# A hybrid decoder trunk in one kernel: the last value pair by halves, value tiles on VectorE, the last round's rows by output weight, and the first weight half split ahead of x

## The reference

```python
z = gelu(x @ w_in + b_in)                 # 1024 -> 2 * 3072, exact gelu
u, v = split(z, 2)
v = layer_norm(v, ln_g, ln_b)             # over all 3072; the last chunk's rows of v are outputs too
sg = chunk_spatial_gate(v, w_s, b_s)      # per chunk of 128 tokens and per head: lower-triangular W_s @ v + b_s
y = (u * sg) @ w_out                      # 3072 -> 1024
x = layer_norm(ALPHA * x + y, ln1_g, ln1_b)
```

## Time and profile before

| what | us |
| --- | --- |
| median of 3 runs | 1261.38 |
| lowest, highest | 1260.33, 1261.75 |
| the profiled execution | 1261.01 |
| its span, first to last instruction | 1259.0 |
| PE busy in it | 1211.5 |
| DVE busy | 908.9 |
| ACT busy | 626.7 |
| POOL busy | 260.8 |

### The profile page before, as it was taken

How to read it: one execution, slowest core, us unless ns; L and a number is a source line. 1 busy time by engine, 2 the same in 40 slices (tenths; PEclk the granted TensorE clock), 3 DMA queues, 4 the chain that set the end, 5 groups by cost and what they waited for, 6 DMA issues and landing times.

```text
span 1259.0 us, 19311 instructions
## 1 busy us (share of the span) xinstructions
PE 1211.5 (96%) x7563; PEld 1094.7 (87%) x7563; DVE 908.9 (72%) x1215; ACT 626.7 (50%) x756; POOL 260.8 (21%) x270
## 2 busy tenths in 40 slices
PE   7999988999999997999999999999999999999998
PEld 6888888999999996888778699999998888877698
DVE  4654788687877875889889786445534889888793
ACT  4332444444444542478888663211221478888651
POOL 2311022442514422022332001000002022232100
PEclk9999999999999998999999999999999999999999
DMA  8456326675957755379999563222422369999512
GB/s 303 146 185 210 118 71 178 144 193 122 204 156 156 192 138 210 143 270 373 372 385 342 194 185 106 70 99 68 134 67 89 143 236 365 381 387 355 213 51 76
DMA packets 99582, 246.47 MB, mean 196 GB/s; under 512 B 10694, under 2 KB 55886, under 8 KB 87216
## 3 DMA queue, kind: packets, MB, share of 16 engines
q1 hardware_dynamic: 68976, 182.20, 40.7%
q0 software_dynamic: 30528, 63.20, 18.1%
HBM read 212.50 MB, written 49.62 MB: 208 GB/s over the span
## 4 chain that ended last, share of the span: by engine, by line
PE 66%; DMA 14%; DVE 11%; ACT 5%; issue 3%; POOL 0%; SPq 0%; DVEq 0%; POOLq 0%; ACTq 0%
PE ps L2073 13%; PE ps L2075 12%; PE ps L2074 12%; DMA w_raw<-in_moe_w_gate_up 9%; PE ps L2124 3%; PE ps L2126 3%; PE ps L2125 3%; DVE w_lo L1382 3%; PE ps L2482 2%; ACT w_hi L981 2%; PE ps L2484 2%; PE ps L2483 2%; PE ps L2175 1%; PE ps L2288 1%; PE ps L2290 1%
## 5 line engine op out<-in xcount | busy, mean ns | idle before, releaser
L1382 DVE TENSOR_TENSOR w_lo<-w_raw,w_hi 128x2048 fp32r<-128x2048 f32 (+1 forms) x133 | 290.4, 2191 | 64.3 <-ACT w_hi L981 57.2
L2073 PE MATMUL ps<-x_hi,w_hi 128*128 128x288 f32 (+2 forms) x784 | 234.8, 299 | 4.2 <-DVE g_full L1538 2.3
L981 ACT ACTIVATE w_hi<-w_raw 128x2048 fp32r<-128x2048 f32 (+1 forms) x121 | 219.7, 1826 | 36.6 <-PE ps L2075 16.1
L2075 PE MATMUL ps<-x_hi,w_lo 128*128 128x288 f32 (+2 forms) x784 | 232.3, 296 | 0.0
L2074 PE MATMUL ps<-x_lo,w_hi 128*128 128x288 f32 (+2 forms) x784 | 232.2, 296 | 0.0
L2073 PEld LDWEIGHTS ps<-x_hi,w_hi 128*128 128x128 f32 x784 | 148.8, 190 | 6.2 <-issue 4.9
L2074 PEld LDWEIGHTS ps<-x_lo,w_hi 128*128 128x128 f32 x784 | 148.9, 190 | 0.1
L2075 PEld LDWEIGHTS ps<-x_hi,w_lo 128*128 128x128 f32 x784 | 148.8, 190 | 0.0
L2073 PE MATMUL ps<-g_hi,w_hi 128*128 128x288 f32 x384 | 114.6, 298 | 1.6 <-DVE g_lo L1517 0.7
L2075 PE MATMUL ps<-g_hi,w_lo 128*128 128x288 f32 x384 | 113.3, 295 | 0.0
L2074 PE MATMUL ps<-g_lo,w_hi 128*128 128x288 f32 x384 | 113.1, 295 | 0.0
(11 more groups left out here) (347 smaller groups left out, 2656.5 us busy)
## 6 DMA issues: line engine op xcount, KB each, us to landing
w_raw<-in_moe_w_gate_up SPq DMA_DIRECT2D x34, 1024.0 KB
w_raw<-in_moe_w_down SPq DMA_DIRECT2D x32, 1024.0 KB
w_raw_more<-in_moe_w_gate_up SPq DMA_DIRECT2D x30, 1024.0 KB
w_raw<-in_a_w_in SPq DMA_DIRECT2D x23, 1024.0 KB
w_raw<-in_a_w_out SPq DMA_DIRECT2D x12, 1024.0 KB
w_raw<-in_b_w_in SPq DMA_DIRECT2D x12, 1024.0 KB
sum_scratch<-out_stage POOLq DMA_DIRECT2D x40, 288.0 KB, 7.1
w_raw<-in_ple_w_gate SPq DMA_DIRECT2D x8, 1024.0 KB
```

The source lines that it names most:

```text
L981: act.activation(unit_of(whi, d), raw_unit(d), ACT.Copy).then_inc(hi_done, 1)
L1382: dve.tensor_tensor(unit_of(wlo, d), raw_unit(d), unit_of(whi, d).bitcast(f32), ALU.subtract).then_inc(split_done, 1)
L2073: pe.matmul(out, sh, mh, start=first, stop=False)
L2075: ins = pe.matmul(out, sl, mh, start=False, stop=final)
```

## The change

It has four parts.

- **Start.** ScalarE and VectorE split the first half of the first weight unit before x of token tile 0.
- **Last value pair.** TensorE runs the last pair by halves, like pair 0, with its loop over the pairs written out. Its first unit is free after the first half (`wait_used`). ScalarE and VectorE split unit U_A, make its sums and split these at the end of pair 4 instead of in pair 5, and in pair 5 the second unit (U_A + 2) with its sums. ScalarE copies the first product before the square root of the variance.
- **Value tiles.** ScalarE's and POOL's operations on tiles 3 and 4 go in every round; VectorE normalises all five. In round 0 the five stand between the combinations, and the first two spatial products stand together behind the second product of `jj` 1.
- **Last round's rows.** The wait for the second output unit moves behind the products of the first output half of both row tiles; the second half's follow in one piece.

The rest is counts: one increment of `rs_ok` is gone.

```diff
--- before.py
+++ after.py
@@ -555,7 +555,8 @@
             elif d >= 4:
-                eng.wait_ge(vps_done, it * (NT * step // 2) + NT * (d // 2 - 1))
+                n, a = divmod(d - 4, 2)
+                eng.wait_ge(vps_done, it * (NT * step // 2) + (NT * (n + 1) if n < VP - 1 else NT * n + 1 + NT * a))
@@ -864,15 +865,6 @@
-            def v_affine(rnd, i):
-                t, v = tok(i), vc[:, i, :] if i < NT - 1 else vcs[0:TS, :]
-                pool.wait_ge(act_scaled, KT + 2 * rnd + i - 2)
-                ch.link(pool.tensor_tensor(v, v, gb[0:t, 0, :], ALU.mult))
-                pool.tensor_tensor(v, v, gb[0:t, 1, :], ALU.add).then_inc(vn_ok, 1)
-
-            pool.wait_ge(vc_ld, 64)
-            for i in range(3, NT):
-                v_affine(0, i)
             for rnd in range(AR):
@@ -883,10 +875,6 @@
                         add_sum(rnd, mo)
-                        if mo == 3:
-                            pool.wait_ge(vc_ld, 64 * (rnd + 2))
-                            for i in range(3, NT):
-                                v_affine(rnd + 1, i)
@@ -981,6 +969,8 @@
+            act.wait_ge(fh_ld, 16)
+            act.activation(whi[:, 0, 0:UNIT // 2], raw[:, 0, 0:UNIT // 2], ACT.Copy).then_inc(fh_ok, 1)
             for i in range(NT):
@@ -988,8 +978,6 @@
                 if i == 0:
-                    act.wait_ge(fh_ld, 16)
-                    act.activation(whi[:, 0, 0:UNIT // 2], raw[:, 0, 0:UNIT // 2], ACT.Copy).then_inc(fh_ok, 1)
                     act.wait_ge(wld[0], 16)
@@ -1029,16 +1017,15 @@
                         elif i == 0:
-                            first_hi(U_A)
-                        else:
-                            sum_hi(U_A + 1)
+                            first_hi(a_entry(0, 2))
                     k = 3 * n - 3 + (i - 1 if i < 2 else i - 2)
...
                         combined_hi(i - 3)
-                if n == VP - 1:
-                    first_hi(a_entry(0, 2))
+                if n == VP - 2:
+                    first_hi(U_A)
+                    sum_hi(U_A + 1)
@@ -1047,9 +1034,6 @@
                 v_pair(n)
-            act.wait_ge(rs_ok, 1)
-            act.activation(rstd[:, :], rstd[:, :], ACT.Sqrt).then_inc(sq_ok, 1)
-
             def u_gelu(u, part):
@@ -1070,11 +1054,6 @@
-            def v_centred(rnd, i):
-                t, v = tok(i), vc[:, i, :] if i < NT - 1 else vcs[0:TS, :]
-                act.wait_ge(vc_ld, 64 * (rnd + 1))
-                act.activation(v, v, ACT.Identity, bias=nmr[0:t, i:i + 1], scale=rstd[0:t, i:i + 1]).then_inc(act_scaled, 1)
-
             def first_product(u):
@@ -1083,11 +1062,8 @@
                 u = 2 * rnd
-                first_product(u)
-                if rnd == 0:
-                    act.wait_ge(rs_ok, 3)
-                    for i in range(3, NT):
-                        v_centred(0, i)
+                if rnd:
+                    first_product(u)
                 sum_hi(a_entry(rnd, 3))
@@ -1110,13 +1086,14 @@
                         sum_hi(a_entry(rnd + 1, 1))
-                        for i in range(3, NT):
-                            v_centred(rnd + 1, i)
                     if mo == 5:
...
                 act.wait_ge(xi_st[j], 64)
+            first_product(0)
+            act.wait_ge(rs_ok, 1)
+            act.activation(rstd[:, :], rstd[:, :], ACT.Sqrt).then_inc(sq_ok, 1)
             for rnd in range(AR):
...
@@ -1381,6 +1358,11 @@
+            def half_lo(done, c0):
+                dve.wait_ge(done, 1)
+                return dve.tensor_tensor(wlo[:, 0, c0:c0 + UNIT // 2], raw[:, 0, c0:c0 + UNIT // 2], whi[:, 0, c0:c0 + UNIT // 2].bitcast(f32), ALU.subtract)
+
+            half_lo(fh_ok, 0).then_inc(fh_ok, 1)
             for i in range(NT):
@@ -1388,9 +1370,7 @@
                 if i == 0:
-                    for c, s in ((fh_ok, slice(0, UNIT // 2)), (hi_done, slice(UNIT // 2, UNIT))):
-                        dve.wait_ge(c, 1)
-                        dve.tensor_tensor(wlo[:, 0, s], raw[:, 0, s], whi[:, 0, s].bitcast(f32), ALU.subtract).then_inc(fh_ok if c is fh_ok else split_done, 1)
+                    half_lo(hi_done, UNIT // 2).then_inc(split_done, 1)
                 if i == 3:
@@ -1448,7 +1428,7 @@
                         dve.wait_ge(v_st[i // 4], n * 16)
-                    dve.wait_ge(vps_done, NT * n + i + 1)
+                    dve.wait_ge(vps_done, NT * n + i + 1 + (n == VP - 1))
                     ins = dve.tensor_tensor(vst[:, i, :], v_bank(i), v_bias_row(n), ALU.add)
@@ -1456,24 +1436,22 @@
                         lo(2 * n + 2 + i // 2)
-                    if n == VP - 1 and i == 0:
-                        combined_lo(1)
-                    if n == VP - 1 and i in (1, 3):
-                        if i == 1:
-                            first_lo(U_A)
-                            sums(U_A)
-                        else:
-                            lo(U_A + 1)
                     if i >= 1:
                         v_stats(n, i - 1)
+                    if n == VP - 1 and i == 1:
+                        first_lo(a_entry(0, 2))
+                    if n == VP - 1 and i == 2:
+                        sums(a_entry(0, 2))
                     if n == VP - 2 and i < 2:
...
                     combined_lo(0)
-                if n == VP - 1:
-                    first_lo(a_entry(0, 2))
+                    combined_lo(1)
+                    first_lo(U_A)
+                    sums(U_A)
+                    lo(U_A + 1)
@@ -1540,17 +1518,21 @@
                 combined(u, 0)
+                if rnd == 0:
+                    v_norm(0)
                 combined(u, 1)
                 if rnd == 0:
-                    sums(a_entry(0, 2))
+                    v_norm(1)
                 combined(u, 2)
-                if rnd:
+                if rnd == 0:
+                    v_norm(2)
+                else:
                     lo(a_entry(rnd, 3))
...
                 if rnd == 0:
-                    for i in range(3):
-                        v_norm(i)
+                    v_norm(3)
+                    v_norm(4)
                 combined(u, 5)
@@ -1587,7 +1569,8 @@
                 lo(d + 1)
-                v_norm(2)
+                for i in range(2, NT):
+                    v_norm(i)
                 first_lo(d + 2)
@@ -1602,7 +1585,6 @@
             dve.wait_ge(rs_ok, 2)
-            dve.scalar_tensor_tensor(out=nmr[:, :], in0=mv[:, :, 0], scalar=-1.0, in1=rstd[:, :], op0=ALU.mult, op1=ALU.mult).then_inc(rs_ok, 1)
             dve.wait_ge(vc_ld, 64)
...
@@ -2155,10 +2137,16 @@
             small_turns()
-            v_pair(1)
-            with pe.Fori(0, VP // 2 - 1) as it:
-                for j in range(2):
-                    v_pair(2 + j, it, 2)
+            for n in range(1, VP - 1):
+                v_pair(n)
+            for a in range(2):
+                pe.wait_ge(split_done, U_A - 1 + a)
+                for i in range(NT):
+                    if a == 0:
+                        pe.wait_ge(vz_done, NT * (VP - 2) + i + 1)
+                    ins = v_half(VP - 1, a, i)
+                    if a or i == NT - 1:
+                        ins.then_inc(vps_done, 1)
             pe.wait_ge(ones_ok, 1)
@@ -2208,8 +2196,9 @@
                         strassen(rnd, jj, n)
-                        if rnd == 0 and jj and n in (1, 2):
-                            spatial(rnd, n - 1)
+                        if rnd == 0 and jj and n == 1:
+                            spatial(rnd, 0)
+                            spatial(rnd, 1)
                         if jj and n == 4:
@@ -2384,14 +2373,14 @@
                     row_turns(1)
-                    pe.wait_ge(split_done, d + 2)
+                    pe.wait_ge(split_done, d + 1)
                     for k0, k1 in ((0, 2), (2, 3), (3, 4)):
...
                         for i in range(2):
-                            for h in range(2):
-                                ins = row_products(i, h, range(k0, k1))
-                            if k1 == ROUND:
-                                ins.then_inc(mt_done, 1)
+                            row_products(i, 0, range(k0, k1))
+                    pe.wait_ge(split_done, d + 2)
+                    for i in range(2):
+                        row_products(i, 1, range(ROUND)).then_inc(mt_done, 1)
                 p_turns(0)
```

More of the change, by code:

```diff
@@ L1273, in norm @@
                     t = tok(i)
-                    act.wait_ge(rs_ok, 3 + n2 + i + 1)
+                    act.wait_ge(rs_ok, 2 + n2 + i + 1)
                     act.activation(xtok[0:t, i, :], xtok[0:t, i, :], ACT.Identity, bias=nmr[0:t, i:i + 1], scale=rstd[0:t, i:i + 1]).then_inc(nz_ok, 1)
@@ L1633, in norm_of @@
                     ch.link(dve.reciprocal(rstd[0:t, i:i + 1], rstd[0:t, i:i + 1]))
-                    dve.wait_ge(rs_ok, 3 + n1 + i + 1)
+                    dve.wait_ge(rs_ok, 2 + n1 + i + 1)
                     dve.scalar_tensor_tensor(out=xtok[0:t, i, :], in0=xtok[0:t, i, :], scalar=rstd[0:t, i:i + 1], in1=lnp[0:t, 1, :],
```

(4 more changed lines are left out.)

## The result

The median of five runs is 1252.51 us (1251.87 to 1253.47), against 1261.38 for the kernel before, measured beside it: a ratio of 0.9928 [0.9916, 0.9940], 8.9 us less. The forecast was 1252.6. The profiled execution of the kernel after took 1253.47, the slowest of the five, with a span of 1251.4; the traces therefore differ by 7.6 us, 1.3 less than the medians.

A forecast was written before the change was run, and what follows sets the result against it. TensorE, busy 96% of the span, bounds the kernel, plus its stops. 0.8 + 6.2 + 0 + 1.8 = 8.8 us off 1261.01 gives 1252.2, with 0.37 for the median 1252.6; range 1251 to 1254 (45%).

The forecast's parts named there:

- A: Start: splitting the first weight half ahead of x lets TensorE's first product start at 9.2 instead of 10.03, 0.8 us.
- B: Last value pair and round 0: fifth product of the second column starts at 191.9 instead of 198.15, 6.2 us.
- VectorE's new wait of 2 us: Last value pair: VectorE waits 2 us before tile 0's bias, which goes 1.1 us late; its bank isn't needed before 170.
- The two idle pieces: Round 0: TensorE idles 0.95 us before the spatial products and 1.0 us before the next product.
- clock drop: Round 0 rival: the clock falls there as well, 1.65 us lost again, 1254.2; chance 10%.
- The rival in which B's stop only moves: Round 0: sums, tiles and low parts still queue on VectorE; if 4 us later than counted, 1256.6; chance 5%.
- the drain behind a table load: ScalarE's square root: the skill's rule makes the load about 2.66 us, not 1.28, giving 1253.5; prediction said the trace disagrees.
- C: Value tiles, rounds 1 to 5: VectorE's two extra tiles, 2.9 us per round, are covered by its waits; 0 us.
- The slower rival: Rounds 1 to 5: VectorE becomes the bound, 15 us on the path, 1267.6; chance 3%.
- D: Last round's rows: row tile 0 turned at 489.0 instead of 493.51, 4.5 us, less 2.65 for half clock: 1.8 net.
- The rival in which the clock stays up: Last round's rows: no clock drop behind the longer gap, 11.5 us in all, 1249.9; chance 20%.
- The one with the longer slow stretch: Last round's rows: 16 transposes don't bring the clock back and run at half speed; D is 0, 1254.4; chance 17%.

The follow-up runs named there:

- e1: The kernel after with the start as before (first weight half no longer split ahead of x); median 1253.83 us.
- e12: The kernel before with only layer norm's parameters scaled by VectorE instead of POOL, in both layers; median 1261.82 us, ratio 0.9997.
- e3: The kernel before with only the new start and the new order of the last round's rows; median 1258.68 us.
- e10: The kernel after with ScalarE's copy of the first product behind the square root again; median 1254.59 us.
- e4: The kernel after with value tiles 3 and 4 of rounds 1 to 5 on ScalarE and POOL again; median 1252.83 us.
- e5: The kernel after with unused products of ones keeping TensorE running ahead of the turnings of side inputs and row tile 0; median 1251.57 us.
- e7: e6 with TensorE turning row tile 0 ahead of the side inputs; median 1247.69 us.
- e9: e6 with unused identity products on TensorE at the start, three calls before x lands and five behind its transposes; median 1245.84 us.
- e2: The kernel after with the last round's output product waiting for both weight units again; median 1255.09 us.
- e6: The kernel after with layer norm's parameters scaled by VectorE instead of POOL, in both layers; median 1247.06 us.

## Why the prediction was right, step by step

**A, the start: 0.8 predicted, 1.5 in the trace.** The mechanism is as told. ScalarE and VectorE do the half first, and x after it:

```profile
6.10 1.06 ACT L973 ACTIVATE w_hi<-w_raw 128x1024 fp32r<-128x1024 f32 x1 [4.01 <-DMA w_raw<-in_a_w_in]
7.06 1.06 ACT L979 ACTIVATE x_hi<-ps 128x512 fp32r<-128x512 f32 x2
7.19 1.23 DVE L1363 TENSOR_TENSOR w_lo<-w_raw,w_hi 128x1024 fp32r<-128x1024 f32 x1 [7.19 <-ACT w_hi L973]
...
8.33 1.28 DVE L1371 TENSOR_TENSOR x_lo<-ps,x_hi 128x512 fp32r<-128x512 f32 x2
...
9.07 0.80 PE L2106 MATMUL ps<-w_hi,x_hi 128*128 128x512 f32 x1 [2.36 <-DVE x_lo L1371]
```

The first product came at 9.07 (9.2 predicted). The other 0.5 was not in the sum: TensorE starts at half clock (0.63 us for a product of 512 columns, later 0.39), and in the kernel after the clock rose at about 12.4 instead of 14.5. This is read from the matmuls' own times; the column of the granted clock stands at 1.00 from 9 to 16 us in both traces and doesn't show it. I had treated the slow stretch as part of the fixed work. But the extra 0.5 is not the change's. In the nine traces with the new start and nothing added in front, the first product comes at 8.83 to 9.26 and the first sample product at 25.21 to 26.73, on average 26.0. In the three with the old start (before, e1, e12) these are 9.95 to 10.06 and 26.35 to 27.64, on average 27.0. So A is worth 1.0 at both places. What decides when the clock rises no run here shows.

**B, the last pair and round 0: 6.2 predicted, 6.5 in the trace** (8.03 at the fifth product less the start's 1.51), and B and C together 6.2 to 6.7 by e3. The chain:

```profile
157.56 2.29 DVE L1359 TENSOR_TENSOR w_lo<-w_raw,w_hi 128x2048 fp32r<-128x2048 f32 x1 [1.98 <-ACT w_hi L1010]
159.89 0.69 DVE L1432 TENSOR_TENSOR v_stage<-ps,v_bias 128x512 f32<-128x512 f32 x1
```

```profile
183.49 1.16 PE L2163 MATMUL ps<-w_spatial,v_cols 128*128 128x128 f32 x8 [0.61 <-DVE v_cols_sample L1476]
186.42 0.40 PE L2055 MATMUL ps<-x_combined_hi,w_hi 128*128 128x288 f32 x1 [0.43 <-DVE w_lo L1359]
190.12 0.40 PE L2055 MATMUL ps<-x_combined_hi,w_hi 128*128 128x288 f32 x1 [0.23 <-ACT g_full L1061]
```

VectorE's new wait of 2 us at the low part of the sums came (1.98), the bias of tile 0 behind it was late as told (159.89, with everything 1.5 earlier), and nobody needed it. The two idle pieces stand where they were forecast and are half as long (0.61 and 0.43 instead of 0.95 and 1.0). The fifth product of the first column has no wait. No clock drop followed: between 173 and 200 the granted clock is 1.00. The rival in which B's stop only moves is out.

The working had one step on too little: that the trace of before disagrees with the drain behind a table load. Its row has 1.73 us of idle between the load and the root, and a drain of 1.38 would fit into that. A row of the same trace that it didn't use decides it, like e10: the next load ends at 187.56 and the Gelu behind it starts at 187.57.

```profile
186.28 1.28 ACT L1057 ACT_TABLE_LOAD   x1
187.57 0.96 ACT L1057 ACTIVATE g_full<-g_full,cols 128x288 f32<-128x288 f32 x2
```

**C: 0 predicted, nothing measurable (e4).** The slower rival is out: in the window above, TensorE is busy all 250 us and VectorE 188.

**D: 4.5 less 2.65 predicted, 3.8 less 2.5 in the trace.** From the last turning of sums (461.26, 8.19 earlier than before) to the turning of row tile 0 (11.95 earlier) the gain is 3.8. The 0.7 that is missing: the norm starts 0.1 behind the scaling, as I had it, but the parameters landed 0.3 late, and VectorE has 0.39 before its second operation. The clock fell, as the forecast had it, and took back 2.5 (e5), so D brought 1.3 at the router against 1.8.

The rival in which the clock stays up is out, and e5 shows what it would have looked like. The one with the longer slow stretch is half right: the 16 transposes did run at half clock (1.97 and 1.92 us for eight). But they took the place of products in the slow stretch and were not added to it: the clock was back at about 486.8, 5.3 us after the gap, as behind the stop of before, so that the loss is 2.5 us and not 4.5. The rule that this rival went by, that transposes do not bring the clock back, is not borne out: in e7 and in e9 it rose behind sixteen transposes and no product. The start, where the prediction saw it confirmed, couldn't tell, since 3.47 us of idle lie between the transposes and the first product there.

By e2 the medians give D 2.6 to 3.1, with ranges of about 2 us; the traces give 1.3 to 1.5. I don't know which is nearer. What the prediction's step missed is the first of the two waits: it named only POOL's parameters, and the load of the side inputs ends later (477.8), on the same queue. It cost nothing in itself, since the norm was later still, but with it the idle came in two pieces, 3.55 us ahead of the side inputs' eight transposes and 1.71 behind them, and not in one.

The terms come to 1.5 + 6.5 + 0 + 1.3 = 9.3 in place of 8.8, and the traces show 9.5 at the router. That the median lies 0.1 us from the forecast is luck: in these traces A was 0.7 and B 0.3 larger than forecast and D 0.5 smaller, at the end the traces differ by only 7.6, and the medians by 8.9.

## What to carry to other kernels

When a stop goes, ask at once what the engine behind it waits for next, and price that with the clock: here the next one was a 5.4 us operation on POOL that had been free of cost, and moving it was worth nothing that could be measured before the change and over 5 us after it. A gain next to TensorE's idle is paid partly in clock, so look at both of its ends: fill the gap or close it. If the order on one engine changes, go through the queues of the engines that serve it as well. And before a loss in one trace is explained, look at the same stretch in the traces of kernels that don't change it.

## What the runs showed of the hardware

- The same 128x2048 float32 multiplication by a constant took 5.39 us on POOL and 1.17 us on VectorE. The Trainium skill (GPSIMD Engine Reference, 4.1 Engine selection) calls one-input elementwise work on that engine roughly line-rate; here it takes 4.6 times as long as on VectorE. VectorE's wait for it ends 0.13 us behind it, so the length is not only the profile's.
- A sum of 128x512 on VectorE took 0.69 us alone and 1.64 to 1.66 us while POOL worked on value tiles (before, round 0).
- A table load on ScalarE ran ahead of a pending input in the kernels before and after and behind it in e10. What decides this no run here shows. In e10 it put the load's 1.28 us on the path.
- TensorE's clock stayed at 2.4 GHz over gaps of 2.15 us (before) and 2.50 us (e2) and was at 1.2 GHz behind gaps of 2.33 (before, round 0), 2.67 (e9), 2.82 (e7) and 3.33 us (e12, in part). So the length of the gap alone doesn't decide it, and this is no rule, only what was seen.
- Transposes brought the clock back without any product: behind the gaps of e7 and e9, sixteen of them ran at half clock (1.90 to 1.93 us for eight) and the next eight at full (1.07 and 1.08).
- The load of the 64 KB of side inputs took 12.2 (e6), 14.1 (e9) and 15.0 us (after) from issue to landing. The gap in front of their turning was 0.77, 2.67 and 3.55 us in these, and only the first left the clock up. In e9 half of the longer gap is TensorE's earlier arrival. That the landing also makes the range of e6's times (4.5 us) is possible and not shown.
